# Quarter tiles in the delta rule's inverse, and RWKV-7's prepared rows kept in SBUF

## The reference, cut to what matters

```
gc = cumsum(g);  decay = exp(gc_i - gc_j) for i >= j
lmat = strictly_lower((k * beta) @ k.T * decay)
tmat = inverse(lmat + eye)                      # unit lower triangular
u, w = tmat @ (v * beta), tmat @ (k * beta * exp(gc))
per chunk: v_new = u - w @ s
           o = q_in @ s + (q @ k.T * decay) @ v_new
           s = s * exp(g_last) + k_out.T @ v_new
```

## Time and profile before

| | |
|---|---|
| three runs | 3882.69, 3885.30, 3886.67 us; median 3885.3 |
| profiled execution | 3884.71 us, its span 3882.9 us |
| PE, PEld | busy 3510.3 us (90%), 3354.7 us (86%) |
| DVE, POOL, ACT | busy 1904.0 (49%), 1184.6 (31%), 1066.3 us (27%) |
| delta rule's loop | about 385 to 678 us of the span |
| RWKV-7, rows prepared | about 2330 to 2411 us |
| RWKV-7, chunks | about 2411 to 2760 us |

### The profile page before, as it was taken

How to read it: one execution, slowest core, us unless ns; L and a number is a source line. 1 busy time by engine, 2 the same in 40 slices (tenths; PEclk the granted TensorE clock), 3 DMA queues, 4 the chain that set the end, 5 groups by cost and what they waited for, 6 DMA issues and landing times.

```text
span 3882.9 us, 74167 instructions
## 1 busy us (share of the span) xinstructions
PE 3510.3 (90%) x31266; PEld 3354.7 (86%) x31266; DVE 1904.0 (49%) x2436; ACT 1066.3 (27%) x1513; POOL 1184.6 (31%) x560
## 2 busy tenths in 40 slices
PE   8998788799999999989997886777799999999979
PEld 7998787799999999989996444777689999999979
DVE  1562555475454454654412224555467544544564
ACT  2365332242111111141003334222224111111142
POOL 2332532353333333333332000000154333333323
PEclk9999999899999999999998997999999999999989
DMA  3111000311111111112211008221121111111111
GB/s 128 54 57 53 1 0 3 111 60 50 43 43 43 43 43 43 50 49 81 89 66 61 6 0 294 46 43 34 62 66 50 43 43 43 41 42 43 43 45 71
DMA packets 106878, 212.10 MB, mean 55 GB/s; under 512 B 58544, under 2 KB 59824, under 8 KB 106096
## 3 DMA queue, kind: packets, MB, share of 16 engines
q1 hardware_dynamic: 94800, 168.65, 14.2%
q10 hardware_dynamic: 11936, 41.34, 2.8%
HBM read 172.73 MB, written 37.23 MB: 54 GB/s over the span
## 4 chain that ended last, share of the span: by engine, by line
PE 82%; DVE 6%; ACT 5%; issue 4%; POOL 1%; DMA 1%; ACTq 0%; DVEq 0%; SPq 0%; POOLq 0%; PEldq 0%
PE PS L734 56%; PE PS L751 7%; PE PS L1385 6%; PE PS L995 4%; PE PS L766 1%; PE PS L1350 1%; PE PS L1449 1%; ACT XH L1700 1%; ACT Y L1701 1%; DVE XL L2295 1%; PE PS L1328 1%; PE PS L1408 1%; PE PS L1325 1%; PE PS L1310 0%; PE PS L923 0%
## 5 line engine op out<-in xcount | busy, mean ns | idle before, releaser
L734 PE MATMUL PS<-XH,WHI 128*128 128x274 f32 x4320 | 1254.1, 290 | 11.4 <-ACT RN L1586 6.3
L734 PE MATMUL PS<-XL,WHI 128*128 128x274 f32 x4320 | 1253.6, 290 | 0.0
L734 PE MATMUL PS<-XH,WLO 128*128 128x274 f32 x4320 | 1251.6, 290 | 0.0
L849 POOL TENSOR_TENSOR WHI<-RAW,EPS 128x1024 fp32r<-128x1024 f32 x234 | 453.9, 1940 | 2467.7 <-PE PS L734 1419.3
L734 PEld LDWEIGHTS PS<-XH,WHI 128*128 128x128 f32 x4320 | 817.1, 189 | 14.4 <-issue 11.5
L734 PEld LDWEIGHTS PS<-XL,WHI 128*128 128x128 f32 x4320 | 818.7, 190 | 0.0
L734 PEld LDWEIGHTS PS<-XH,WLO 128*128 128x128 f32 x4320 | 818.1, 189 | 0.0
L852 POOL TENSOR_TENSOR WLO<-RAW,WHI 128x1024 fp32r<-128x1024 f32 x234 | 604.6, 2584 | 18.4
L734 PE MATMUL PS<-HH,WHI 128*128 128x274 f32 x1280 | 372.0, 291 | 0.0
L734 PE MATMUL PS<-HH,WLO 128*128 128x274 f32 x1280 | 370.4, 289 | 0.0
L734 PE MATMUL PS<-HL,WHI 128*128 128x274 f32 x1280 | 369.5, 289 | 0.0
(11 more groups left out here) (445 smaller groups left out, 5704.9 us busy)
## 6 DMA issues: line engine op xcount, KB each, us to landing
RAW<-in_units SPq DMA_DIRECT2D x234, 512.0 KB, 3.6
prepared_rows<-PREP SPq DMA_DIRECT2D x8, 1096.0 KB, 6.0
CIN<-prepared_rows SPq DMA_DIRECT2D x17, 512.0 KB, 4.4
c_rows<-DX ACTq DMA_DIRECT2D x14, 548.0 KB, 2.8
RKV<-c_rows SPq DMA_DIRECT2D x4, 1644.0 KB, 9.9
X<-in_x SPq DMA_DIRECT2D x8, 548.0 KB, 9.7
XR<-in_x ACTq DMA_DIRECT2D x8, 548.0 KB, 11.6
bonus_gate_rows<-BG SPq DMA_DIRECT2D x4, 1096.0 KB, 5.4
```

The source lines that it names most:

```text
L734: last = nc.tensor.matmul(PS[:, 4 * slot + b, 0:width], wt[:, ring, w], r[:, k, b * width:(b + 1) * width], start=n == 0, stop=n == 3 * nk ...
L849: nc.gpsimd.tensor_tensor(WHI[:, s, :], RAW[:, s, :], ZERO.to_broadcast([128, 1024]), ALU.add)\
```

## The change

**Quarter tiles.** A chunk of the delta rule has 128 tokens, so the lower triangular matrix of a head has two 64x64 blocks on the diagonal and one below them. Levels 1 to 5 only touch the diagonal blocks. They now live in tiles [128, 4, 64] (names with _B): the upper block in partitions 0 to 63, the lower one in 64 to 127, and their products go through `c_heads`. Level 6 joins the two halves: one product of the block below the diagonal with the lower inverse, and one with the upper, four 64x64 matmuls each, and the results are packed into TT, whose other half is zeroed once. The masks are compacted once into BLOCK_LEVEL. The block below the diagonal is written by a step of its own ("below") ahead of the transposition's result; POOL masks five levels, no longer six; ACT packs the diagonal blocks in step w6.

**Prepared rows.** kk, k, kka and the log decay stay in SBUF for all tokens (KK4, K24, KKA4, SIG4), no longer in PREP and DRAM. The running sum is taken in the stage that prepares the rows, three scans for each group m over 64, 512 and 512 columns, and prep0 has no scan. CIN holds eight rows for each chunk. Since BONUS4 and GATE4 share the space of KK4 and K24, their loads move behind the last read of those, near the end of the chunk loop.

```diff
-        TA, TT, WW, VB, KO, RR, VN = [pair(x, 7 + n) for n, x in enumerate(("TA", "TT", "WW", "VB", "KO", "RR", "VN"))]
+        TT, VB, KO, RR, VN = [pair(x, n) for x, n in (("TT", 8), ("VB", 10), ("KO", 11), ("RR", 12), ("VN", 13))]
+        BLOCK_LEVEL = at("BLOCK_LEVEL", [128, 6, 64], spare)
+        TT_B = [at("TT_B%d" % p, [128, 4, 64], spare + 1536 + 1024 * p) for p in range(2)]
...
@@ POOL
-                    nc.gpsimd.tensor_tensor(LM[p][:, :, :], DB[p][:, :, :], heads_of(level_mask(l)), ALU.mult).then_inc(s, 1)
+                    nc.gpsimd.tensor_tensor(LM_B[p][:, :, :], DB_B[p][:, :, :], pairs_of(BLOCK_LEVEL[:, l, :]), ALU.mult)\
+                        .then_inc(s, 1)
-                elif name[0] == "w" and name != "w6":
+                elif name[0] == "w" and int(name[1]) < 5:
@@ PE
-                    pe.wait_ge(gdn_dve[p], G_DVE.at(j, "m0"))
-                    turned(b + 1, LM[p]).then_inc(s, 1)
+                    pe.wait_ge(gdn_dve[p], G_DVE.at(j, "below"))
+                    tiled()
+                    c_heads(stacked(b + 1), LM_B[p], PAIR_ID).then_inc(s, 1)
...
-                    by_head(b + 1, LM[p], TT[p]).then_inc(s, 1)
+                    if l < 6:
+                        pe.wait_ge(gdn_pool[p], G_POOL.at(j, "m%d" % l))
+                        tiled()
+                        c_heads(stacked(b + 1), LM_B[p], TT_B[p]).then_inc(s, 1)
+                    else:
+                        tiled()
+                        for m in range(4):
+                            last = nc.tensor.matmul(stacked(b + 1)[half(0), m, :], DB[p][half(1), m, half(0)], TT_B[p][half(1), m, :],
+                                                    start=True, stop=True)
+                        last.then_inc(s, 1)
...
-                    by_head(b + 2, TA[p], WW[p]).then_inc(s, 1)
+                    tiled()
                     if l < 6:
-                        by_head(b + 3, WW[p], TA[p]).then_inc(s, 1)
+                        c_heads(stacked(b + 2), TA_B[p], WW_B[p]).then_inc(s, 1)
+                        c_heads(stacked(b + 3), WW_B[p], TA_B[p]).then_inc(s, 1)
...
                 elif name == "carry1":
                     pe.wait_ge(gdn_dve[p], G_DVE.at(j, "r"))
+                    pe.wait_ge(gdn_act[p], G_ACT.at(j, "packed"))
@@ PE, RWKV-7, prep2
-                    pe.wait_ge(c_dve[p], C_DVE.at(j, "scan"))
+                    pe.wait_ge(c_in[p], 32 * j[0] + 32 + 32 * j[1])
@@ ACT, RWKV-7, prep0
-                    act.wait_ge(c_dve[p], C_DVE.at(j, "scan"))
-                    nc.scalar.activation(PX[p][:, :, 1:65], CIN[p][:, 12:16, :], ACT.Exp, scale=-DECAY).then_inc(s, 1)
+                    if not starts_set(j):
+                        act.wait_ge(c_dve[p], C_DVE.before(j))
+                    decay = SIG4[:, :, chunk_columns(j, p)]
+                    nc.scalar.activation(PX[p][:, :, 1:65], decay, ACT.Exp, scale=-DECAY).then_inc(s, 1)
...
@@ DVE, RWKV-7, rows prepared
                 nc.vector.tensor_tensor(kka, kk, kka, ALU.mult).then_inc(e_dve, 1)
-            for p in range(2):
-                dve.wait_ge(e_out[p], 96)
+                for t0, n in ((S0, 64), (P0, 512), (P0 + 512, 512)):
+                    x = SIG4[:, m, t0:t0 + n]
+                    last = nc.vector.tensor_tensor_scan(x, RUN[:, 0:n], x, 0.0, ALU.mult, ALU.add)
+                last.then_inc(e_dve, 1)
```

More of the change, by code:

```diff
@@ L381, in build @@
         WG = room("WG", [128, 2, NT])
-        RKV, PREP, BG, NORM = both("RKV", 3, NT), both("PREP", 4, NT), both("BG", 2, NT), both("NORM", NT)
-        K2R, SIGR, KKR, KKAR, BONUSR, GR = 0, 1, 2, 3, 0, 1
+        RKV, NORM = both("RKV", 3, NT), both("NORM", NT)
+        RUN = room("RUN", [128, 512])
+        TAIL = SLAB // 32 * 32
+        KK4, K24 = at("KK4", [128, 4, NT], 0), at("K24", [128, 4, NT], 8 * TILE)
+        KKA4, SIG4 = at("KKA4", [128, 4, NT], TAIL - 12 * TILE), at("SIG4", [128, 4, NT], TAIL - 8 * TILE)
+        BG = [at("BG%d" % p, [128, 2, NT], TAIL - (4 - 2 * p) * TILE) for p in range(2)]
+        assert place[0] <= TAIL - 12 * TILE, (place[0], TAIL - 12 * TILE)
+        BONUSR, GR = 0, 1
         place[0] = AR
-        RUN = room("RUN", [128, 256])
         MB = [room("MB%d" % n, [128, 4, 64]) for n in range(2)]
         behind_states = place[0]
-        CIN = both("CIN", 24, 64)
+        CIN = both("CIN", 8, 64)
         ARI = both("ARI", 4, 192)
@@ L505, in before @@
                 return i * self.count + 1
-        def level_mask(l):
-            return small("level", 128, 128 * l)
         def heads_of(x):
@@ L832, in _ @@
             load_tokens(0, chunk_columns(C_SAMPLE, 0))
+            for p in range(2):
+                sp.wait_ge(e_out[p], 32)
+            sp.wait_ge(c_dve[0], C_DVE.at(C_SAMPLE, "kb"))
+            sp.wait_ge(c_dve[1], C_DVE.at((0, 7), "kb"))
+            for rows4, first, n in ((BONUS4, 0, 0), (GATE4, 4, 1)):
+                sp.dma_start(rows4, BROW.rearrange("(k m) p n -> p (k m) n", m=4)[:, first:first + 4, :]).then_inc(mix_in[n], 16)
             load_units(OUT_UNIT[1] // 2 + 2, NU // 2)
@@ L991, in _, with c_heads, tiled @@
             pe.wait_ge(norm_root, 8)
+            def c_heads(out, lhs, rhs, more=()):
+                terms = [(lhs, rhs)] + list(more)
+                for m in range(4):
+                    for n, (l, r) in enumerate(terms):
+                        for h in range(2):
+                            x = r[half(h), :] if len(r.shape) == 2 else r[half(h), m, :]
+                            last = nc.tensor.matmul(out[half(h), m, :], l[half(h), m, :], x,
+                                                    start=n == 0, stop=n == len(terms) - 1)
+                return last
+            def tiled():
+                pe.sem_inc(c_turn, 1)
             def by_head(bank, lhs, rhs, start=True, stop=True):
@@ L1376, in _ @@
                 back(i, *order[-1])
-            def c_heads(out, lhs, rhs, more=()):
-                terms = [(lhs, rhs)] + list(more)
-                for m in range(4):
-                    for n, (l, r) in enumerate(terms):
-                        for h in range(2):
-                            x = r[half(h), :] if len(r.shape) == 2 else r[half(h), m, :]
-                            last = nc.tensor.matmul(out[half(h), m, :], l[half(h), m, :], x,
-                                                    start=n == 0, stop=n == len(terms) - 1)
-                return last
-            def tiled():
-                pe.sem_inc(c_turn, 1)
             def c_step(name, j, p):
@@ L1627, in g_step @@
                     act.wait_ge(gdn_pe[p], G_PE.at(j, name))
-                    nc.scalar.activation(WW[p][:, :, :], per_head(b + 1), ACT.Copy).then_inc(s, 1)
+                    rows_of = slice(0, 128) if name != "w6" else half(0)
+                    nc.scalar.activation(WW_B[p][rows_of, :, :], stacked(b + 1)[rows_of, :, :], ACT.Copy).then_inc(s, 1)
+                    if name == "w6":
+                        act.wait_ge(gdn_dve[p], G_DVE.at(j, "tt5"))
+                        for h in range(2):
+                            last = nc.scalar.activation(TT[p][half(h), :, half(h)], TT_B[p][half(h), :, :], ACT.Copy)
+                        last.then_inc(s, 1)
                 elif name == "carry1":
@@ L2143, in _ @@
             dve.wait_ge(row_out[1], 112)
+            for h in range(2):
+                nc.vector.tensor_copy(BLOCK_LEVEL[half(h), :, :],
+                                      small("level", 6 * 128).rearrange("p (l c) -> p l c", l=6)[half(h), :, half(h)])
+            dve.wait_ge(norm_done, 10)
+            for p in range(2):
+                nc.vector.memset(TT[p][half(1), :, half(0)], 0.0)
             step(nc.vector.memset(SP[:, :, :], 0.0))
@@ L2610, in c_step @@
                 level = int(name[1:]) if name[0] in "wt" else 0
[L2611 to L2617 removed]
+                r = CIN[p][:, 0:4, :]
+                kk, k, kka = [x[:, :, chunk_columns(j, p)] for x in (KK4, K24, KKA4)]
+                if name == "prep1":
                     dve.wait_ge(c_act[p], C_ACT.at(j, "pi"))
@@ L2701, in _ @@
                 nc.vector.tensor_copy(ARI[p][:, :, 128:192], pairs_of(PAIR_ID))
+            for p in range(2):
+                dve.wait_ge(e_out[p], 32)
             nc.vector.memset(CO[:, :, 0:S0], 0.0)
```

91 lines of the change are left out of this document (47 added, 44 removed).

## The result

The changed kernel takes 3847.2 us (median of four runs, 3846.2 to 3849.5) against 3886.0: a ratio of 0.9903, 95% interval 0.9888 to 0.9918. The direction was right; 3847.2 lies at the upper end of the range, 25 us above the forecast. The profiled executions stand 38.1 us apart (spans 3882.9 and 3844.8). Five marks divide that; the timelines of both kernels have them.

A forecast was written before the change was run, and what follows sets the result against it. PE was taken to set the delta rule's pace, and RWKV-7's chunks' only together with others (DVE's scan in the chain). Savings of 44 + 16 + 2 = 62 us from 3884.7 gave a forecast of 3822 us, range 3797 to 3848.

The forecast's parts named there:

- Quarter products: Delta rule: 0.46 us from start to start for 0.90; twelve on the path save 5.2 us of a period.
- Rival (e): Delta rule: quarter products between whole ones take 0.9 us again, only shorter evacuations stay; 3856 us, chance 0.05.
- Array changes: Delta rule: PE's switch between quarter and whole tiles costs 0.19 us, five on the path, +0.95 us a period.
- rival (a): Delta rule: switches between quarter and whole tiles are dear, 0.5 us each; 3839 us, chance 0.13.
- From the sums of decays to the transposition: Delta rule: DVE and ACT set the time, PE's saving is worth nothing; -0.3 us of 9.31.
- One slow stretch for 1.3 us in every period: Delta rule: PE at the lower clock behind the transposition once a period, 1.3 us, making the period 25.8.
- the 24.5: Delta rule: period in us at full clock after the change, 5.0 less than 29.5.
- rival (d): Delta rule: PE stays at the lower clock throughout, since it idles longer in each period; 3952 us, chance 0.04.
- The last half alone and the first: Delta rule: last chunk's second half, running alone, gains 4.4 us; first chunk's first half gains 1.
- RWKV-7's chunks: Without the scan, w4's copy follows its product: 1.0 us of 18.75 for sixteen periods, -16 us.
- The stage before: Row preparation before RWKV-7's chunks: -6.0 us behind the last row, +3.9 for scans lengthening the groups; -2 us.
- Rival (b): Scans only move: row groups 2.8 us longer each, half of RWKV-7's gain goes; 3835 us, chance 0.10.

The follow-up runs named there:

- g_fill: Changed kernel with four PE products that nothing reads in each delta rule period, ahead of three waits: 3847.2 us, ratio 0.9904.
- g_pool: Changed kernel with POOL's mask of the decays held back until DVE has started TA: 3837.2 us, ratio 0.9874.
- g_rr: Changed kernel with v_new's right-hand side formed by four DVE instructions, one for each head, in place of two: 3841.0 us, ratio 0.9887.
- c_unroll: Changed kernel with PE's loop over RWKV-7's chunks written out: 3820.7 us, ratio 0.9842.
- b_unroll: Kernel before the change with PE's loop over RWKV-7's chunks written out: 3865.4 us, ratio 0.9956 to the kernel before.
- before_pad66: Kernel before the change with 66 empty PE instructions behind the delta rule's loop: 3889.7 us, ratio 1.0018.

## Why the prediction was wrong, point by point

**Quarter products: right.** 0.46 to 0.51 us from start to start, evacuations 0.38 and 0.42. Rival (e) is out.

**Array changes: small, and below my 0.19.** Whole products behind a quarter one start 0.61 us after it (607.31 to 607.92), quarter behind quarter 0.46 to 0.51: 0.10 to 0.15 a change. The fillers of g_fill add changes and the period falls; rival (a) is out.

```profile
607.31 0.68 PE L1005 MATMUL PS<-TT_B,LM_B 64*64 64x64 f32 x16
607.92 1.16 PE L1015 MATMUL PS<-KT 128*128 128x128 f32 x8
```

**From the sums of decays to the transposition: failed, 0.4 us of a period.** The sum had -0.3 us of 9.31; it is 9.38 (606.25 to 615.63). What failed is the path. I let DVE and ACT set the time there, put PE's saving at nothing and took 0.85 us from the last step before the exponentials. That step did shrink (0.43), but the chain of waits doesn't pass through it in either kernel: it runs through PE's products up to t4 and from there to DVE's beta product. Before:

```profile
511.40 1.80 PE PS L995 x16
...
513.84 0.88 DVE DB L2168
```

After:

```profile
610.41 1.10 PE PS L1005 x32
...
611.87 1.35 DVE DB L2204
```

So the quarter products bring the beta product 1.05 us nearer to the sums (5.62 us behind them, 6.67 before), but there DVE meets POOL's other mask: 1.34 us for 0.87. From its end to the transposition it takes 2.42 us for 1.77, near the sum's terms for the new steps. g_pool shows what the meeting costs: without it the path is 8.7 us. Where the sums run at the slow clock (three of the last seven times), the beta product runs alone and the path is 10.3 us; that belongs to the slow clock below.

**The wait before v_new: not in the sum, 0.65 us.** It was 0.8 us and I put its change at nothing, without a reason. DVE's second step now takes 1.02 us on the mean beside the next POOL mask, for 0.69; the rest would be that PE comes there sooner. g_rr shows that this wait lies on the period's path.

**One slow stretch for 1.3 us in every period: failed, 0.7 us.** The price was not too low, the count was: a stretch costs 1.0 to 1.1 us (periods of 25.5 with none, 26.6 with one, 27.6 to 27.8 with two), but the last six periods have ten of them, counting the double one as two. At clock 1.00 the period is 25.5 (g_fill, c_unroll), which is 24.5 + 0.4 + 0.65 of the points above; so the slow clock costs 2.0 us of 27.5. That the 24.5 fits so well is in part luck: array changes came out cheaper than its terms and quarter products up to 0.05 us dearer. My rival (d) named the mechanism and priced only its extreme; the window's clock is 0.90. The three sum to 1.75 us for each of eight periods, the 14 us that the delta rule lacks.

**The last half alone and the first:** from the last sums to the product behind the loop 6.0 us less (forecast 4.4); the first sums come 0.4 later.

**RWKV-7's chunks: mechanism right, term failed.** The copy of w4 follows its product (0.72 us behind its start, 1.59 before: 2568.00 to 2569.59), the chain lost 0.8 to 0.9 us for 1.0. What the step took for granted is that each period is the undisturbed one, 18.75 us, and that the loop's other costs stay. They are 20.1 us on the mean before and 19.5 after. Of the 16 us the change itself gives 9.7 (b_unroll to c_unroll, to the output norm), and 6.0 are left as timed. The loop's place explains the step from one to the other: the kernel before at the changed kernel's place (before_pad66) takes 355.6 us from the first exponential to the output norm, for 350.7, and against it the change brings 10.9 us. What else makes the last chunk longer is open.

```profile
2673.80 0.68 PE L1005 MATMUL PS<-TT_S,LM_S 64*64 64x64 f32 x16
2674.52 0.39 ACT L2004 ACTIVATE W_S<-PS 128x256 f32<-128x256 f32 x1 [1.57 <-PE PS L1005]
```

**The stage before: better, by 5 us.** The groups start 22.1, 13.2 and 14.4 us apart, for 21.2, 12.3 and 12.9, 3.2 us more in all, close to the +3.9; but the last group takes 3.5 us less to its last row, so from the first prepared row to the last it takes 59.2 us (59.5 before). The scans, 2.5 us for the three of a group, filled DVE's waits, and by that mark the +3.9 was 0. From the last prepared row to the exponential 4.2 us (10.8 before; 4.8 forecast). Rival (b) is out. Bonus and gate rows were not waited for.

```profile
2372.30 1.30 DVE L2730 TENSOR_TENSOR KKA<-KK,KKA 128x1096 f32<-128x1096 f32 x1
2373.52 2.52 DVE L2734 TENSOR_TENSOR_SCAN SIG<-RUN,SIG 128x64 f32<-128x64 f32 x3
```

## What to carry to other kernels

Look at idle time put down to "issue" at a loop's jump before costing any edit ahead of that loop: its price depends on where the code lies, and an edit elsewhere moves it. Before a stretch is said to be set by some engines, follow the chain of waits through it. Where an engine gets faster between waits that stay, count the slow-clock work behind each wait, and try cheap fillers. A DVE step slowed by POOL is not healed by shortening one of POOL's steps; see which step DVE reaches next.

## What was not expected of the hardware

Position alone changed the stalls of one loop of 1800 PE instructions between two and six of six jumps (3.0 to 5.0 us each), and writing the loop out, six copies of it more, left none of them. An empty PE instruction cost 0.13 us in a row of 164. Products that nothing reads, 4.2 us of them in a period, made it 2 us shorter.
